# One step of a two-layer decoder: the load of the gate weights moves behind the second half of the new tokens in ScalarE's load queue

## The reference, cut to what matters

```python
proj = x @ w_in                                  # x (tokens, 1024), w_in (1024, 3088)
q, k, v, o, g = jnp.split(proj, [512, 1024, 2048, 3072], axis=-1)
g = g.astype(F32) + b_gate.astype(F32)           # 16 columns: 8 input gates, 8 forget gates
ig = g[..., :8]
lf = jax.nn.log_sigmoid(g[..., 8:])
h, state = mlstm_chunkwise(q, k, v, ig, lf, C0, n0, m0)
h = jax.nn.sigmoid(o) * h.reshape(B, L, 1024)
return h @ w_out, state
```

## Time and profile before

| | us |
|---|---|
| median of 3 executions | 899.94 |
| the three | 899.6, 899.94, 902.54 |
| the profiled execution, whole | 902.97 |
| its span, from first to last instruction | 901.2 |
| TensorE busy in it | 887.2 |
| VectorE busy | 626.4 |
| ScalarE busy | 439.8 |
| mean granted clock of TensorE, as a share of full speed | 0.996 |

### The profile page before, as it was taken

The page is one execution under the profiler, slowest core; times in us unless marked ns, Lnnn a source line. Parts: engine busy times, 40 slices in busy tenths (PEclk is TensorE's granted clock), DMA queues, the critical chain, the costliest instruction groups (busy, mean ns, idle before and its releaser), DMA issues.

```text
span 901.2 us, 18722 instructions
## 1 busy us (share of the span) xinstructions
PE 887.2 (98%) x7472; PEld 839.8 (93%) x7472; DVE 626.4 (70%) x1092; ACT 439.8 (49%) x826; POOL 65.0 (7%) x83
## 2 busy tenths in 40 slices
PE   8999999999999999999999999999999999999996
PEld 8999998999999999999988788988999999999985
DVE  6477669788976575677666857447568797747536
ACT  5445667476355363445444453345547634526321
POOL 0010007400000000330000000000230000000000
PEclk9999999999999999999999999999999999999999
DMA  9983215654454444566998898998945455554401
GB/s 285 259 257 102 95 48 140 207 179 149 148 172 142 141 146 162 167 219 229 327 327 292 326 396 305 400 407 332 290 140 176 153 158 178 152 167 141 141 1 59
DMA packets 132331, 182.78 MB, mean 203 GB/s; under 512 B 5875, under 2 KB 113211, under 8 KB 132244
## 3 DMA queue, kind: packets, MB, share of 16 engines
q1 hardware_dynamic: 126938, 177.56, 59.6%
q10 hardware_dynamic: 4666, 1.92, 0.8%
q0 software_dynamic: 640, 2.10, 0.7%
HBM read 175.24 MB, written 6.32 MB: 201 GB/s over the span
## 4 chain that ended last, share of the span: by engine, by line
PE 94%; DVE 2%; ACT 2%; issue 1%; DMA 1%; ACTq 0%; SPq 0%; DVEq 0%
PE ps L639 24%; PE ps L641 23%; PE ps L640 23%; PE ps L1041 6%; PE ps L1141 3%; PE ps L1083 3%; PE ps L929 1%; PE ps L931 1%; DMA raw<-in_w_in_a_dram 1%; PE ps L930 1%; PE ps L653 1%; PE ps L756 0%; PE ps L1014 0%; PE ps L823 0%; PE ps L940 0%
## 5 line engine op out<-in xcount | busy, mean ns | idle before, releaser
L1258 ACT ACTIVATE w_hi<-raw 128x1024 fp32r<-128x1024 f32 x192 | 202.3, 1056 | 224.3 <-PE ps L641 200.2
L1665 DVE TENSOR_TENSOR w_lo<-raw,w_hi 128x1024 fp32r<-128x1024 f32 x192 | 238.9, 1247 | 101.6 <-ACT w_hi L1258 101.5
L639 PE MATMUL ps<-x_hi,w_hi 128*128 128x322 f32 (+1 forms) x888 | 279.3, 315 | 0.0
L641 PE MATMUL ps<-x_hi,w_lo 128*128 128x322 f32 (+1 forms) x888 | 276.1, 311 | 0.0
L640 PE MATMUL ps<-x_lo,w_hi 128*128 128x322 f32 (+1 forms) x888 | 275.7, 311 | 0.0
L639 PE MATMUL ps<-h_hi,w_hi 128*128 128x320 f32 x552 | 170.7, 309 | 0.0
L641 PE MATMUL ps<-h_hi,w_lo 128*128 128x320 f32 x552 | 170.3, 308 | 0.0
L640 PE MATMUL ps<-h_lo,w_hi 128*128 128x320 f32 x552 | 170.3, 308 | 0.0
L639 PEld LDWEIGHTS ps<-x_hi,w_hi 128*128 128x128 f32 x888 | 167.9, 189 | 1.7 <-issue 1.0
L640 PEld LDWEIGHTS ps<-x_lo,w_hi 128*128 128x128 f32 x888 | 168.5, 190 | 0.2
L641 PEld LDWEIGHTS ps<-x_hi,w_lo 128*128 128x128 f32 x888 | 167.4, 188 | 0.0
(11 more groups left out here) (349 smaller groups left out, 979.8 us busy)
## 6 DMA issues: line engine op xcount, KB each, us to landing
raw<-in_w_up_dram SPq DMA_DIRECT2D x32, 1024.0 KB, 5.7
raw<-in_w_down_dram SPq DMA_DIRECT2D x32, 1024.0 KB, 5.2
page<-in_cache_k_dram SPq DMA_DIRECT2D x64, 512.0 KB, 5.7
page<-in_cache_v_dram SPq DMA_DIRECT2D x64, 512.0 KB, 9.6
raw<-in_w_in_a_dram SPq DMA_DIRECT2D x11, 1024.0 KB, 8.7
raw<-in_w_kv_dram SPq DMA_DIRECT2D x8, 1024.0 KB, 5.3
raw<-in_w_out_a_dram SPq DMA_DIRECT2D x4, 1024.0 KB, 5.2
raw<-in_w_q_b_dram SPq DMA_DIRECT2D x4, 1024.0 KB, 5.3
```

The source lines that it names most:

```text
L639: mm(out, WH[PLACE[t]][:, k, :], hi[:, k, 0:width], start=(k == 0), stop=False)
L641: last = mm(out, WL[PLACE[t]][:, k, :], hi[:, k, 0:width], start=False, stop=(k == 7))
L1258: A(WH[PLACE[t]][:, :, :], raw_tile(t), ACT.Copy)\
L1665: V.tensor_tensor(WL[PLACE[t]][:, :, :], raw_tile(t), WH[PLACE[t]][:, :, :].bitcast(F32), ALU.subtract)\
```

## The change

The three loads on ACT's queue go out in another order: first half of the new tokens, second half, gate weights, where it was first half, gate weights, second half. Loads, sizes, semaphores and all waits are the same.

```diff
@@ -1270,7 +1270,7 @@
             for i in range(2):
                 c = slice(512 * i, 512 * i + 512)
                 act.dma_start(XS[0:64, 2, c], x_sample.rearrange("b t c -> (b t) c")[:, c]).then_inc(s_xs[i], 16)
-                if i == 0:
+                if i == 1:
                     act.dma_start(wgraw[:, :, :], lhs_k(win[:, 3072:3088])).then_inc(s_gw, 16)
             nc.scalar.preload_act_table_set("natural_log_exp_and_others")
             act.wait_ge(s_gw, 16)
```

## The result

| | before | changed |
|---|---|---|
| median, us (16 executions each) | 901.33 | 902.75 |
| lowest to highest | 899.6 to 902.66 | 900.36 to 905.35 |
| the profiled execution, whole | 902.97 | 902.07 |

The account below looks back on a forecast made before the run. TensorE, busy 887.2 of 901.2 us, was taken as the bound, with only its early waits movable. Half, gate weights and weight tile each added 0: 902.97 us for the profiled execution, 900.0 as median, range 899.1 to 902.7 us.

Parts of the forecast that it names:

- The second half, earlier: New tokens' second half, issued at 1.38 instead of 2.00 us, lands at 4.2 us; TensorE's chunk 4 gains 0.
- The gate weights, later: Gate weights' load on ScalarE's queue, issued 0.62 us later, takes 4.65 us again, lands at 6.7 us and costs 0.
- The upper bound of 5.8 us: Gate weights' load takes what the earlier load in that place took: landing at 7.8 us, cost 0.2 us.
- the far bound of 9.4: Gate weights' load takes 7.41 us like the first weight tile's: landing at 9.4 us, cost 1.8 us.
- The room, 1.55 us: ScalarE's idle times before weight tile 0's high part, 0.29, 0.44 and 0.82 us, can absorb a later gate-weights landing.
- The forecast's 7.6: Latest gate-weights landing, in us, that leaves the chain untouched: 6.03 + 1.55.
- Handed on one for one: A shift of TensorE's restart at 12.82 us reaches the end in full; past the room each microsecond costs one.
- The second, the new wait: Gate weights land after 7.6 us and ScalarE delays TensorE: 0.2 to 1.8 us slower, up to 901.7 us; chance 0.18.
- The third, the clock: TensorE idles before the gate products and its clock falls, 1.2 us; with the late load 902.9 us; chance 0.05.
- The first, faster because the weight tile moves up: Small packets out of the prompt's way speed SP's queue; gain ends at 0.82 us, 899.1 us; chance 0.13.
- The base: Starting time for the forecast median: 899.94 us, median of three executions, with a 3 us spread between executions.

Follow-up runs that it names:

- e1: Changed load order, with ScalarE making the gate weights' high part behind chunks 0 and 1 and VectorE their low part behind chunk 1; 901.81 us, ratio 1.0003.
- e2: Changed kernel plus 11 unused matmuls in TensorE's holes ahead of chunks 4 and 6 and chunk 6's gate product; 903.21 us, ratio 1.0022.
- e6: Changed load order, gate weights replaced by another 64 KB block in 128 pieces of 512 bytes instead of 1024 of 64; 901.68 us, ratio 1.0007.
- e10: Kernel before, unaltered, run for a second profile; 901.8 us in one execution.
- e5: Kernel before with its own load order, ScalarE made to wait for the prompt's last quarter before starting on the gate weights; 902.15 us, ratio 1.0023.
- e3: Kernel before with the gate weights' load first on ScalarE's queue, then both halves of the new tokens; 901.62 us, ratio 1.0004.
- e8: Changed kernel once more, unaltered, beside other variants on the same chip; 902.36 us, ratio 1.0025.
- e9: Kernel before, its loads kept: all chunks turned before gate products, ScalarE's chunks 6, 7 before weight tile 0, tile 1's bank emptied earlier; 900.07 us, ratio 0.9983.
- e4: Changed order with the gate weights' load placed behind ScalarE's function-table load, but issued only 0.03 us later than in the changed kernel; 901.73 us, ratio 1.001.

## Why the prediction was wrong, and where it was right

**The second half, earlier: right, worth 0.** Its landing was off (5.8 to 6.6 us in the three profiles, not 4 to 5), and where chunk 4 waited, it was for the prompt's third quarter.

**The gate weights, later: this is the step that failed.** The prediction said: "I take the row of the same load, 4.65 us, which gives 6.7 us ... It costs 0." So it took the load's time from issue to landing as a property of the load, and set its cost to nothing. In the new place the load took 5.5, 6.8 and 7.0 us, and 6.2 and 6.5 in the two experiments that kept the loads of the change (e1, e2). The upper bound of 5.8 us, a landing at 7.8, was exceeded in four of these five; the far bound of 9.4 held. The assumption behind it was that the 1024 small packets set the duration by themselves. They do count (e6), but two things come on top. They begin to move 1.5 us later for an issue 0.6 us later; the prediction held the second half's bytes ahead of them to cost "the same 0.6 us that the later issue costs, so I don't add it". And once begun they take longer, in 5 to 8 us instead of 3 to 5. From 6 us on SP's queue moves more beside them, 0.25 to 0.34 MB in a microsecond against 0.13 to 0.25 in 3 to 5; that this is the reason is argued. The prediction had seen that the half took 5.8 us in that place, put it down to the 1024 small packets ahead of it, and so argued against a landing as late.

**The room, 1.55 us: a number of one execution.** It was added from the idle times of a profile in which the weight tile landed at 10.83 us. The rule that held in all six profiles is simpler: the gate weights may land until 3.0 us before the weight tile does. That is 7.8 us for that profile, 0.2 more than the sum of the idle times, but 7.1 for e10's, where the tile landed at 10.1. The forecast's 7.6 lies between, and was not the weak point.

**Handed on one for one: right.** ScalarE's start on the tile and TensorE's on tile 0 are 2.8 us apart in five of six profiles. From there to the end the rest is the same within 0.4 us in the five profiles without the fall near 44 us. The wait alone costs no less than the change (e5), and moving the wait alone undoes the loss (e1). The weight tile's load was not touched by the change: 10.5 to 10.9 us, against 10.1 to 10.8 before.

**The rivals.** The second, the new wait "of up to 1.8 us", came true: its price is 0 in the first profile, 1.3 and 1.4 in the two others; it had been given a chance of 0.18. The prediction set a rule of the Trainium skill beside it (DMA: Bandwidth & Descriptors, "Rules for kernel authors": issue early, wait late). Waiting later agrees with it (e1, the loss is gone); issuing earlier than before gained nothing here (e3, 1.0004). The third, the clock, came true as an addition in one profile of three, at 1.1 us against the 1.2 forecast, from a landing at 9.05 us against the 9.1 forecast; with one execution that agreement may be luck. The first, faster because the weight tile moves up, did not come: the tile landed no earlier.

**The base.** The forecast was 900.0 us, up to 902.7 at most. It took 899.94 us, a median of three, as the median of the kernel. Over 16 executions it is 901.33. Of the 2.8 us between 899.94 and 902.75 one half, 1.4, is the base, and the other what the change costs. The prediction knew that its profiled execution was 3.0 us over that median and did not ask why. A large part of it is in the earlier trace rows: the fall of the clock near 44 us is in some executions and not in others, and behind tile 0 those with it take 1.1 to 2.7 us more (the two groups above). The prediction had priced such a fall at 1.2. In e8 it is absent (the stretches of 2 us, in order):

```profile
44.00:46.00 2.00, 2.00 (x20) 1.89 (x20) 0.51 (x7) 0.76 (x1) 0.00 (x0) 1.00 0.89 283
46.00:48.00 2.00, 2.00 (x16) 2.00 (x15) 2.00 (x7) 0.00 (x0) 1.39 (x1) 1.00 0.45 146
```

Sorted by the mean clock of the whole execution, the kernel before has a mean time of 900.03 us at 0.999 (21 executions) and 901.41 at 0.997 (28); the changed kernel 900.94 (4) and 902.45 (8). At these clocks the change costs 0.9 and 1.0 us, but 1.5 at 0.996 (12 executions before, 4 changed) and 2.0 at 0.995 (6 and 6). Its mean clock is also a little lower, 0.9966 over 24 executions against 0.9974 over 76, which fits with a fall near 12 us in some of them. That the two are cause and effect was seen in one trace only. The sorting is a rough one, as it puts several chips together and the mean clock tells nothing of the place of a fall: the five profiles without the fall near 44 us have mean clocks from 0.999 down to 0.995.

What stays open: why the same load in the same place takes 5.5 us in one execution and 7.0 in another, how often the clock falls at 12 us, and whether a late tile 0 makes the fall near 44 us rarer. Of the five profiles with tile 0 at 14.3 us or later one has that fall, of the nine with an earlier one eight; if this is more than chance, it gives back a part of what the change costs.

## What to carry to other kernels

Ask of a load not what it waits for but who waits for it first, and keep it ahead of loads that are needed later, above all when it comes in small pieces and another queue is about to be busy. A landing time read in one place of a queue does not hold for another place; price the new place by the worst load that went through it, and compare room and landing over several profiles where the margin is a microsecond. If a wait can't be made earlier, move it on the waiting engine behind work that is ready (e1), or take work out of the way of the chain (e9).

## What the runs showed of the hardware that was not expected

- One load of 64 KB in 1024 pieces, in one place of the queue, landed 5.5 to 7.0 us after its issue between executions; the load of before, one place earlier, 4.4 to 5.3 in six profiles. Its pieces began to move at 4.75 to 5.0 us instead of 3.25 to 3.5, for an issue 0.6 us later.
- A DMA issue that stands behind the load of an activation table in ScalarE's list went out 0.04 us after the table load had begun, not behind its 1.28 us (e4).
- The granted clock of TensorE near 44 us fell to about half over 3 to 4 us in all three profiles of the kernel before and in one of three of the changed kernel; in the other two it stayed at 1.00. From tile 0 to the end the nine profiles of this case with that fall took 886.3 to 887.6 us, the five without it 884.9 to 885.2.
